# One more projection block between the last attention heads: six whole weight units in six steps

## The reference, cut to what matters

```
u = rms_norm(x, g_mix[1]);  mem_n = rms_norm(mem, g_mem[1])
h = u @ w_in_moba            # 1024 x 2560: q, k, v of 768 columns each, then 256 columns qm
q, k: 12 heads of 64, rms-normalised per head, times a gain, then rotated by position
s = q k^T / 8, causal mask, softmax, times v            # 12 heads
mo = softmax(norm(qm) norm(k_mem)^T / 8) v_mem          # 4 heads on the memory, no mask
x = x + concat(tok, mo) @ w_out[1];  then the MLP of the layer
```

## Time and profile before

| | |
|---|---|
| median of 3 runs | 815.34 us |
| the profiled execution: time / span | 814.75 / 812.9 us |
| PE busy (share of span) | 798.4 us (98%) |
| DVE, ACT, POOL busy | 538.1, 415.6, 112.7 us |
| mean granted TensorE clock | 0.998 of full |

### The profile page before, as it was taken

The page is one execution under the profiler, slowest core; times in us unless marked ns, Lnnn a source line. Parts: engine busy times, 40 slices in busy tenths (PEclk is TensorE's granted clock), DMA queues, the critical chain, the costliest instruction groups (busy, mean ns, idle before and its releaser), DMA issues.

```text
span 812.9 us, 11157 instructions
## 1 busy us (share of the span) xinstructions
PE 798.4 (98%) x4190; PEld 664.5 (82%) x4190; DVE 538.1 (66%) x728; ACT 415.6 (51%) x586; POOL 112.7 (14%) x144
## 2 busy tenths in 40 slices
PE   8999999999999999999999999999899999999998
PEld 6998987778878778888888888887567888888886
DVE  5647988767585766566656556677975766665661
ACT  5546556554655554364444444545665545444440
POOL 1600300000020510030000000079900000000000
PEclk9999999999999999999999999999999999999999
DMA  8951444346747633646655655464214466655541
GB/s 314 322 191 40 156 156 156 119 156 223 241 145 238 208 106 104 207 156 207 206 191 175 202 194 172 151 206 131 78 53 156 156 207 211 209 199 190 175 151 52
DMA packets 76503, 140.43 MB, mean 173 GB/s; under 512 B 2953, under 2 KB 22609, under 8 KB 76465
## 3 DMA queue, kind: packets, MB, share of 16 engines
q1 hardware_dynamic: 74352, 134.03, 49.8%
q0 software_dynamic: 1968, 5.82, 2.3%
q10 hardware_dynamic: 144, 0.07, 0.0%
HBM read 138.86 MB, written 1.05 MB: 172 GB/s over the span
## 4 chain that ended last, share of the span: by engine, by line
PE 90%; DVE 5%; ACT 2%; DMA 1%; issue 1%; POOL 0%; SPq 0%; ACTq 0%; DVEq 0%
PE bank L1737 56%; PE bank L2093 13%; PE bank L2095 7%; PE bank L1885 2%; PE bank L1803 2%; PE bank L2097 2%; DVE w_lo L1176 2%; PE bank L1946 2%; PE bank L1772 1%; PE bank L1855 1%; PE bank L1920 1%; DMA raw<-in_w_in 1%; DVE tok L1348 1%; PE bank L1751 1%; DMA raw<-in_w_mem_kv 1%
## 5 line engine op out<-in xcount | busy, mean ns | idle before, releaser
L1737 PE MATMUL bank<-w_hi,a_both 128*128 128x512 f32 (+2 forms) x752 | 233.6, 382 | 0.4 <-PE bank L1737 0.4
L1176 DVE TENSOR_TENSOR w_lo<-raw,w_hi 128x2048 fp32r<-128x2048 f32 (+2 forms) x65 | 146.0, 2247 | 53.8 <-ACT w_hi L725 53.3
L1615 DVE TENSOR_TENSOR w_lo<-raw,w_hi 128x2048 fp32r<-128x2048 f32 x48 | 110.0, 2292 | 91.9 <-ACT w_hi L1075 91.0
L2093 PE MATMUL bank<-a_both,w_hi 128*128 128x512 f32 x448 | 161.4, 399 | 0.0
L1737 PEld LDWEIGHTS bank<-w_hi,a_both 128*128 128x128 f32 x752 | 140.7, 188 | 22.0 <-issue 1.1
L725 ACT ACTIVATE w_hi<-raw 128x2048 fp32r<-128x2048 f32 (+2 forms) x64 | 120.7, 1888 | 59.7 <-PE bank L1737 35.6
L1075 ACT ACTIVATE w_hi<-raw 128x2048 fp32r<-128x2048 f32 x48 | 92.1, 1918 | 112.5 <-PE bank L1737 53.7
L1737 PE MATMUL bank<-w_hi,b_hi 128*128 128x512 f32 x376 | 148.7, 395 | 0.1
L1737 PE MATMUL bank<-w_hi,b_lo 128*128 128x512 f32 x376 | 146.5, 390 | 0.0
L1737 PE MATMUL bank<-w_lo,b_hi 128*128 128x512 f32 x376 | 146.5, 390 | 0.0
L1737 PE MATMUL bank<-w_lo,a_both 128*128 128x512 f32 (+2 forms) x376 | 141.7, 377 | 0.0
(11 more groups left out here) (242 smaller groups left out, 859.6 us busy)
## 6 DMA issues: line engine op xcount, KB each, us to landing
raw<-in_w_ff SPq DMA_DIRECT2D x64, 1024.0 KB, 5.1
raw<-in_w_in_moba SPq DMA_DIRECT2D x20, 512.0 KB, 4.4
raw<-in_w_merge SPq DMA_DIRECT2D x8, 1024.0 KB, 5.1
raw<-in_w_out SPq DMA_DIRECT2D x8, 1024.0 KB, 5.1
m<-in_w_in SPq DMA_DIRECT2D x6, 880.0 KB, 9.1
raw<-in_w_in SPq DMA_DIRECT2D x5, 880.0 KB, 8.5
raw<-in_w_mem_kv SPq DMA_DIRECT2D x4, 1024.0 KB, 5.2
raw<-in_w_ple_gate SPq DMA_DIRECT2D x4, 1024.0 KB, 5.0
```

The source lines that it names most:

```text
L1176: dve.tensor_tensor(w_lo[:, v % RING, 0:n], landing[land_slot(v)][:, 0:n], w_hi[:, v % RING, 0:n].bitcast(F32), ALU.subtract).then_inc(lo_ ...
L1615: dve.tensor_tensor(w_lo[:, (base + c) % RING, :], raw[:, (base + c) % RAW, :], w_hi[:, (base + c) % RING, :].bitcast(F32), ALU.subtract). ...
L1737: ins = pe.matmul(banks[t][:, 0:n], xa[:, kt, ts], wa[:, slot, w], start=first and k == 0 and q == 0, stop=last and k == kts - 1 and q == 2)
L2093: pe.matmul(b_hid[f][:, :].rearrange("p (q n) -> p q n", q=2), w_hi[:, slot, w], both_, start=kt == 0, stop=False)
```

## The change

Only two blocks (four units) are now multiplied ahead of the steps, and six whole units, `U_MOBA + 2` to `U_MOBA + 7`, fill steps 14 to 19, one in each. The pieces are dealt out anew over the blocks: (k0, memq1) first, then (q0, q1), and as fills (q2, k1), (k2, v0), (v1, v2). The order of `NORMED` follows: memq1, k0, q0, q1, k1, q2, k2; ACT now squares q0 and q1 too, right after the last block ahead of the steps, and DVE reduces them in step 14 behind the maxima. k1 and q2 are squared at the end of step 15, k2 at the end of step 17 (before, k1 and q2 ahead of the steps and k2 in step 16). On DVE the low part of a unit (`unit`) moves from the end of a step to the next step, right behind the maxima. In steps 15, 17 and 19 PE transposes q and k of the next pair (16, 18, 20: `LATE_PARTS`) not behind the logits but before the last part of the fill, and ACT copies them behind the exponentials and `copy_pt`. The waits are adapted to that. ACT's order at the end of a step (evac, squares, then `unit`) stays.

```diff
-MOBA_FILL = {14: (0,), 15: (1,), 16: (2, range(0, 2)), 17: (2, range(2, 4)), 18: (3, range(0, 2)), 19: (3, range(2, 4))}
+MOBA_FILL = {14 + i: i for i in range(6)}
+LATE_PARTS = (16, 18, 20)
-SQUARES_AT = {16: (("k2", B_MOBA + 2),)}
-SQUARES_BY_ACT = ["k1", "q2", "k2"]
-
-MOBA_BLOCKS = [(0, 3), (1, 9), (2, 4), (5, 6), (7, 8)]
+SQUARES_AT = {15: (("k1", B_MOBA + 1), ("q2", B_MOBA + 1)), 17: (("k2", B_MOBA + 2),)}
+SQUARES_BY_ACT = ["q0", "q1", "k1", "q2", "k2"]
+
+MOBA_BLOCKS = [(3, 9), (0, 1), (2, 4), (5, 6), (7, 8)]
...
-NORMED = ["memk1", "memk0", "memq0", "q0", "k0", "memq1", "q1", "k1", "q2", "k2"]
+NORMED = ["memk1", "memk0", "memq0", "memq1", "k0", "q0", "q1", "k1", "q2", "k2"]
... ACT, last_step(n)
-                if n + 1 in RUN3:
+                if n + 1 in RUN3 and n + 1 not in LATE_PARTS:
                     copy_qk(n + 1)
                 exps(n, (0,))
...
                 if n - 1 in RUN3:
                     copy_pt(n - 1)
+                if n + 1 in LATE_PARTS:
+                    copy_qk(n + 1)
... ACT, ahead of the steps
             unit(U_MOBA + 1)
+            copy_qk(RUN3[0])
             block_done(U_MOBA + 1)
             evac(B_MOBA)
-            unit(U_MOBA + 2)
-            unit(U_MOBA + 3)
-            copy_qk(RUN3[0])
-            block_done(U_MOBA + 3)
-            evac(B_MOBA + 1)
-            head_squares("k1", B_MOBA + 1)
-            head_squares("q2", B_MOBA + 1)
+            head_squares("q0", B_MOBA)
+            head_squares("q1", B_MOBA)
... DVE, last_step(n)
                 maxima(n)
+                if n == RUN3[0]:
+                    head_squares("q0", B_MOBA)
+                    head_squares("q1", B_MOBA)
+                for u, k, half_, ks in fill_of(n - 1):
+                    if n - 1 in RUN3 and u < U_MOBA + 7 and 3 in ks:
+                        unit(u)
                 if n - 1 in RUN3:
                     copy_pt(n - 1)
... (and at the end of the step)
-                for u, k, half_, ks in fill_of(n):
-                    if 3 in ks and u < U_MOBA + 7:
-                        unit(u)
... PE, qk_parts(n)
-                if n - 3 >= N_IDX:
-                    pe.wait_ge(pt_cp_v, n - 3 - N_IDX + 1)
+                copied = n - 2 if n in LATE_PARTS else n - 3
+                if copied >= N_IDX:
+                    pe.wait_ge(pt_cp_v, copied - N_IDX + 1)
... PE, transposes(n)
-                pe.wait_ge(qk_cp, min(n + 2, last) + 1)
+                pe.wait_ge(qk_cp, min(n + (1 if n + 2 in LATE_PARTS else 2), last) + 1)
... PE, last_step(n)
                 logits(n)
-                if n + 1 in RUN3:
+                late = n + 1 in LATE_PARTS
+                if n + 1 in RUN3 and not late:
                     qk_parts(n + 1)
+                (fill_,) = fill_of(n)
                 if n - 2 in RUN3:
                     values(n - 2)
-                (fill_,) = fill_of(n)
-                if n - 2 in RUN3:
                     transposes(n - 1)
+                    one_fill(fill_, {2: lambda: qk_parts(n + 1)} if late else ())
+                elif n - 1 in RUN3:
+                    one_fill(fill_, {2: lambda: transposes(n - 1), 3: lambda: qk_parts(n + 1)})
+                else:
                     one_fill(fill_)
-                else:
-                    one_fill(fill_, {2: lambda: transposes(n - 1)} if n - 1 in RUN3 else ())
```

More of the change, by code:

```diff
@@ L148, in fill_of @@
     if n in MOBA_FILL:
-        return [unit_of(U_MOBA + 4, B_MOBA + 2, *MOBA_FILL[n])]
+        return [unit_of(U_MOBA + 2, B_MOBA + 1, MOBA_FILL[n])]
     if n in OUT_FILL:
@@ L706, in _ @@
             rstd(6, D, NT, EPS)
-            norm_and_rotate("q0")
             query_power("memq1").then_inc(memq_made, 1)
-            for what in ("k0", "q1", "k1", "q2", "k2"):
+            for what in ("k0", "q0", "q1", "k1", "q2", "k2"):
                 norm_and_rotate(what)
@@ L1695, in _ @@
             evac(B_MOBA0)
-            head_squares("q0", B_MOBA0)
+            head_squares("memq1", B_MOBA0)
             head_squares("k0", B_MOBA0)
             dense(U_MOBA, B_MOBA)
[L1699 to L1703, removed]
             for n in steps_of(RUN3):
@@ L1849, in qk_parts @@
                 if kind[:3] == "mem":
-                    blocks_read((B_POOL, B_MOBA)[int(kind[3])])
+                    blocks_read((B_POOL, B_MOBA0)[int(kind[3])])
                     pe.wait_ge(memk_made, 2)
@@ L1875, in logits @@
                 kind, pr = kind_of(n), n - N_IDX
+                if n == RUN3[1]:
+                    blocks_read(B_MOBA)
                 pe.wait_ge(qk_cp, n + 1)
@@ L2181, in _ @@
             dense(U_MOBA0, B_MOBA0, a_hi, a_lo, upper(G_MIX1, x, x_half, X_FF0 + 2))
-            dense(U_MOBA, B_MOBA, a_hi, a_lo)
-            dense(U_MOBA + 2, B_MOBA + 1, a_hi, a_lo, ((), {1: lambda: qk_parts(RUN3[0])}))
+            dense(U_MOBA, B_MOBA, a_hi, a_lo, ((), {1: lambda: qk_parts(RUN3[0])}))
             for n in steps_of(RUN3):
```

## The result

The changed kernel takes 817.85 us (median of 20 runs, 815.38 to 820.02), the kernel before 816.1 (20 runs in the same comparison, 814.67 to 818.36). The ratio is 1.0023, with a 95% interval of 1.0013 to 1.0032: 0.23% slower, which is real, but less than the 0.5% that was set as the bound of no change. The profiled execution of the changed kernel took 815.38 us, span 813.6. Forecast were 817.2 and no change.

A forecast was written before the change was run, and what follows sets the result against it. PE, holding 90% of the last chain, bounds the kernel. Losses of 1.4 + 4.0 + 1.7 + 1.1 = 8.2 us against 6.1, plus 0.1 for order, give +2.2: forecast 817.2 us, range 812.3 to 820.8.

The forecast's parts named there:

- Step 14, no wait: At the end of step 14, pair 15's exponentials come just in time: 0 to 0.5 us, taken as 0.
- Step 15: Before the late transposes of q and k, PE waits 1.4 us for DVE's copy; bounds 0 and 2.5.
- the 5.2 us of its other estimate: Normalise beside POOL under the port lock: four instructions each wait 1.3 us, making the sum 1 us higher.
- Step 16: Before the second half of transposes(15), PE waits 4.0 us for ACT's copy_qk(17); lower bound 2.3 to 2.5, upper 5.
- ACT's bare list: Step 16's lower bound: ACT's list takes 5.7 us if DVE evacuates at once, leaving a wait of 2.3 to 2.5.
- The clock: Low clock after the waits of 1.4 and 4.0 us: price 0 to 5.8 us, taken as 1.7.
- Rival 2: Low clock through step 16's whole fill, 24 matmuls at half speed: 5.8 us instead of 1.7, 821.1 us; chance 0.13.
- Steps 17 to 19: No wait in 17; 1.1 us in 18 (0.8 to 2) before transposes(17); 0 to 0.5 in 19.
- The sum: Whole kernel: losses of 8.2 us against 6.1, plus 0.1 for the order, so +2.2 us.
- Two of the signs that the prediction named: Right if the clock is near 0.5 behind step 16's gap; wrong if the difference arises outside 542 to 602.
- 6.1 us to win: Steps 16 to 18 before: removable losses of 0.81, 2.25 and 1.35 us in gaps plus 1.7 of low clock.

The follow-up runs named there:

- e3: Changed kernel, but in step 15 DVE copies pair 14's transposed probabilities out of the shared bank ahead of the low part; 818.49 us, ratio 1.003.
- e1: Changed kernel, but ACT makes a unit's high part in the next step, behind its copy of q and k; 812.95 us, ratio 0.9956.
- e5: Changed kernel without POOL's rotation of q1 (only its factor computed, heads 4 to 7 left unrotated); 814.19 us, ratio 0.999.
- e8: Changed kernel with one more ACT instruction, a copy of 128x1536, ahead of its copy of q and k of pair 17; 819.34 us, ratio 1.0033.
- e6: Kernel before, with only DVE's low part of a unit moved behind the maxima of the next step; 810.82 us, ratio 0.9941.
- e10: Changed kernel with DVE's low part of a unit back at the end of the step, ahead of the next maxima; 818.57 us, ratio 1.0025.
- e2: Changed kernel with both the high part and the squares of k1, q2, k2 moved behind ACT's copy of q and k; 814.0 us, ratio 0.9973.
- e7: Changed kernel without late transposes: q and k of pairs 16, 18, 20 are transposed right behind the logits; 817.97 us, ratio 1.0018.
- e9: As e2, with DVE's reductions of k1 and q2 (k2) also moved behind the maxima of step 16 (18); 815.14 us, ratio 0.9989.
- e4: Changed kernel with the edits of e2 and e3 together; 814.61 us, ratio 0.9978.

## Why the prediction was right

- **Step 14, no wait:** right, 543.47 to 550.73 without a gap.
- **Step 15:** 1.4 us, measured 0.96 of idle time; normalise took 4.0 us where 4.2 was taken, so the 5.2 us of its other estimate did not come. That DVE's copy is the cause is shown by e3.
- **Step 16:** 4.0 us, measured 3.52, by the mechanism named: e1, e5 and e8 each changed one item of the sum and the wait followed (1.73, 2.17, 4.89). The excess over ACT's bare list is POOL's rotation beside DVE's normalise (e5).
- **The clock:** 1.7 us, measured 0 in the profiled execution. The price itself is borne out by the variants. Four of the five traces with a wait of 3.2 to 4.9 us in step 16 have the low level right behind it, and lose 1.7 to 2.9 us there; the changed kernel's own trace is the fifth (the table in the last section). The Trainium skill (TensorE: Matmul & The Clock Gate, Part 1) says that the point at which the clock changes varies from run to run. The traces fit that, with a wait of 3.23 us followed by the low level and one of 3.52 not, but they are of different kernels and show it for no single one. Rival 2, the low clock through the whole fill, stays without support: even behind 4.89 us the loss is 2.9 us, not 5.8.
- **Steps 17 to 19:** 0, 1.1 and 0 us, measured 0, 0.82 and 0.
- **The sum:** +2.2 us, measured 817.85 - 816.1 = 1.75 on the medians.

That the sum came so near is in part luck. The clock term was the same 1.7 us on both sides, so the forecast of +2.2 rested on waits growing by 2.1 us, from 4.4 to 6.5. They grew by 0.9, to 5.3: the terms of steps 15, 16 and 18 were each 0.3 to 0.5 us too large. The other 0.8 us or so of the medians is in none of the terms. It may be clock, since 14 of the 20 runs of the changed kernel are at a mean clock of 0.996 or less, and of the kernel before 28 of the 70 runs whose clock is on record; where in the program it falls in them is not known. Two of the signs that the prediction named also speak against it in the profiled execution: the clock was not near 0.5 behind the gap of step 16, and the difference to the execution before arose ahead of 542 us.

What the prediction did not see is that the change has two parts of opposite sign. It reckoned with 6.1 us to win and gave them to the longer steps and the maxima together. e6 shows that the maxima alone win 5.4 us in the old order, and e10 that in the new order they win next to nothing. The new order, both with maxima first, costs 817.85 - 810.82 = 7.0 us. Of these 4.3 are waits, 5.3 us against 1.0. The rest, 2.7, is not separated further; e6's runs are at 0.998 to 1.000, four of six at 1.000, so clock is the likely part.

## What to carry to other kernels

Where one bank is shared, as here, the copy that frees it can hold PE; add up everything that stands ahead of it in its engine's list, and put what nobody waits for soon behind it. Moving more than that can only move the wait: with the squares moved too (e2), the median was 1.0 us higher than with the high part alone (e1). More work per step covers a latency only if it doesn't lengthen that list. When an edit has several parts, try each alone on the old kernel: here one line of order was worth more than the rearrangement around it.

## What was not expected of the hardware

Whether a wait is followed by the low clock is not settled by its length. These are the traces of the new order in which PE waits before the second half of the transposes in step 16. The third column runs from the end of the wait to the next logits, the same work in every row.

| trace | wait, us | from its end to the next logits, us | mean clock there |
|---|---|---|---|
| e1 | 1.73 | 6.05 | 1.00 |
| e5 | 2.17 | 6.04 | 1.00 |
| e7 | 3.23 | 7.70 | 0.78 |
| changed kernel | 3.52 | 6.05 | 1.00 |
| e10 | 4.00 | 8.40 | 0.70 |
| e3 | 4.56 | 7.94 | 0.74 |
| e8 | 4.89 | 8.91 | 0.66 |

Waits of 2.25 us (the kernel before) and 2.09 us (e9), both in front of step 17's work, were followed by it too. Elsewhere, the granted clock is below 1.00 only in the first 14 us, in five of the twelve traces, and near the end of e6's (0.97 in the 10 us from 800). e2 and e4, whose single waits are at most 1.6 us, have none in the stage.

The runs of one program differ in their mean clock: the changed kernel's groups at a mean clock of 0.998, 0.996 and 0.994 lie at 816.8, 817.9 and 819.6 us, a spread wider than the effect of the change. The clock isn't the whole of the spread, for three runs of the kernel before are at 1.000 and still take 816.26 to 817.75 us. With 1.8 us less of waits, e1 has a median 4.9 us lower.
